# Distance slopes folded into the query scale and the fused add and maximum, in a two-block transformer forward pass

## The reference, cut to what matters

```python
def alibi_slopes(n_heads):
    return jnp.exp2(-8.0 * jnp.arange(1, n_heads + 1, dtype=jnp.float32) / n_heads)
# diff_attention
    sc = jnp.einsum('bqhmd,bkhmd->bhmqk', qi, k).astype(jnp.float32) * scale
    dist = jnp.abs(qpos[:, None] - kpos[None, :]).astype(jnp.float32)
    p = jax.nn.softmax(sc - slopes * dist, axis=-1)
    a = p[:, :, 0] - lam * p[:, :, 1]
# window_attention
    sc = jnp.where(valid, sc - slopes * dist.astype(jnp.float32), -jnp.inf)
```

## Time and profile before

| what | value |
|---|---|
| median of 3 runs | 2623.48 us (2622.71 to 2624.72) |
| the profiled execution: time, span | 2622.06 us, 2620.3 us |
| busy: PE, DVE, ACT, POOL | 2349.5 us (90%), 902.4 (34%), 518.4 (20%), 1046.5 (40%) |
| granted TensorE clock, mean | 0.975 |
| chain that ended last, by engine | PE 72%, DMA 14%, DVE 9%, issue 2% |
| POOL's high parts L480, low parts L483 | x216, 421.9 us; x222, 548.8 us |
| POOL's slope tables L529 (da), L533 (wa) | x8, 19.6 us; x16, 20.7 us |

### The profile page before, as it was taken

How to read it: one execution, slowest core, us unless ns; L and a number is a source line. 1 busy time by engine, 2 the same in 40 slices (tenths; PEclk the granted TensorE clock), 3 DMA queues, 4 the chain that set the end, 5 groups by cost and what they waited for, 6 DMA issues and landing times.

```text
span 2620.3 us, 26993 instructions
## 1 busy us (share of the span) xinstructions
PE 2349.5 (90%) x11209; PEld 1528.1 (58%) x11209; DVE 902.4 (34%) x1264; ACT 518.4 (20%) x1111; POOL 1046.5 (40%) x508
## 2 busy tenths in 40 slices
PE   5999988999998998889899999699988888888886
PEld 5777766888787875566578888343323333232322
DVE  2664855555302026655413353211010111101012
ACT  2253542211102014456411102000000000000001
POOL 5545754888778774444068886000000000000000
PEclk9999998999999999999999999799999999999998
DMA  4211221222222231111012227599999999999996
GB/s 163 80 49 65 81 97 64 97 97 97 97 97 82 97 97 33 33 65 49 1 65 97 97 97 282 238 418 417 417 417 417 416 417 416 417 417 418 418 417 276
DMA packets 172915, 531.60 MB, mean 203 GB/s; under 512 B 10018, under 2 KB 92155, under 8 KB 139515
## 3 DMA queue, kind: packets, MB, share of 16 engines
q1 hardware_dynamic: 169008, 521.17, 51.2%
q10 hardware_dynamic: 3787, 8.71, 0.9%
HBM read 525.66 MB, written 4.19 MB: 202 GB/s over the span
## 4 chain that ended last, share of the span: by engine, by line
PE 72%; DMA 14%; DVE 9%; issue 2%; ACT 1%; POOL 1%; ACTq 0%; SPq 0%; DVEq 0%; POOLq 0%
DMA arena<-in_w_exp_up 9%; PE ps L2062 9%; PE ps L1402 7%; PE ps L1404 7%; PE ps L1403 7%; PE ps L2035 7%; PE ps L1714 5%; DMA ring<-in_w_exp_up 4%; PE ps L1993 2%; PE ps L1418 2%; PE ps L1419 2%; PE ps L1420 2%; PE ps L1490 2%; PE ps L1492 1%; PE ps L1491 1%
## 5 line engine op out<-in xcount | busy, mean ns | idle before, releaser
L480 POOL TENSOR_TENSOR w_hi<-ring,one 128x1024 fp32r<-128x1024 f32 x216 | 421.9, 1953 | 481.7 <-PE ps L1404 179.3
L483 POOL TENSOR_TENSOR w_lo<-ring,w_hi 128x1024 fp32r<-128x1024 f32 x222 | 548.8, 2472 | 29.5 <-ACT w_hi L639 12.6
L579 POOL TENSOR_TENSOR arena<-arena 128x512 f32<-128x512 f32 x8 | 8.4, 1048 | 810.9 <-PE ps L2005 794.2
L1402 PE MATMUL ps<-h_hi,w_hi 128*128 128x512 f32 x656 | 255.9, 390 | 0.8 <-DVE arena L1234 0.8
L1404 PE MATMUL ps<-h_hi,w_lo 128*128 128x512 f32 x656 | 255.5, 389 | 0.0
L1403 PE MATMUL ps<-h_lo,w_hi 128*128 128x512 f32 x656 | 255.4, 389 | 0.0
L2035 PE MATMUL ps<-ring,arena 128*64 128x512 f32 x944 | 213.1, 595 | 41.6 <-DMA ring<-in_w_exp_up 40.1
L2035 PE MATMUL ps<-arena 128*64 128x512 f32 x944 | 213.0, 595 | 41.0 <-DMA arena<-in_w_exp_up 41.0
L2035 PEld LDWEIGHTS ps<-arena 128*64 128x64 f32 x944 | 71.5, 137 | 179.2 <-issue 178.9
L2035 PEld LDWEIGHTS ps<-ring,arena 128*64 128x64 f32 x944 | 71.2, 137 | 178.9 <-issue 176.8
L917 ACT ACTIVATE arena<-ps 64x1024 f32<-64x1024 f32 x32 | 30.8, 1010 | 568.1 <-PE ps L2035 568.1
(11 more groups left out here) (329 smaller groups left out, 4117.7 us busy)
## 6 DMA issues: line engine op xcount, KB each, us to landing
ring<-in_w_exp_gate SPq DMA_DIRECT2D x59, 1024.0 KB, 24.1
ring<-in_w_exp_up SPq DMA_DIRECT2D x59, 1024.0 KB, 25.4
arena<-in_w_exp_gate SPq DMA_DIRECT2D x59, 1024.0 KB, 24.1
arena<-in_w_exp_up SPq DMA_DIRECT2D x59, 1024.0 KB, 25.4
arena<-in_w_exp_down SPq DMA_DIRECT2D x54, 1024.0 KB, 18.7
ring<-in_w_exp_down SPq DMA_DIRECT2D x52, 1024.0 KB, 22.0
ring<-in_w_in SPq DMA_DIRECT2D x34, 1024.0 KB, 5.1
ring<-in_ffn_w_up SPq DMA_DIRECT2D x22, 1024.0 KB, 5.0
```

The lines of the kernel that those rows point to most:

```text
L480: nc.gpsimd.tensor_tensor(hi, w, one[:].unsqueeze(2).to_broadcast(list(w.shape)), ALU.mult).then_inc(w_high, 1)
L483: nc.gpsimd.tensor_tensor(lo, w, hi.bitcast(f32), ALU.subtract).then_inc(w_split, 1)
L1402: mm(o, w[0][:, k, :], h[0][:, k, 0:ntok], start=(k == 0), stop=False)
```

## The change

The score of a head is divided by the head's slope before, by a factor on the queries, and the fused instruction computes (score + (-distance)) times slope. In `da` the factor 0.125/slope is a constant of the eviction L765; in `wa` an eviction holds two heads (64 rows each), so its factor comes from a new tile `wq_scale`, filled by 16 memsets on DVE at the start. The tables of distances are read as they are; the sign of the subtraction and of the mask's fill is turned. The slope tables, their waits on POOL, and the calls of `split` between them go. The two distance tables are made one after the other, four halves later in POOL's order than the first was; behind them comes one `split(NH)` for all that is left. DVE waits for a table once per stage.

```diff
--- before.py
+++ after.py
@@ -43,6 +43,14 @@
 WA_UNIT = [[(i, 2 * qh + i // 2, kb) for i in range(4) for kb in WA_KB[2 * qh + i // 2]] for qh in range(2)]
 
 
+def da_slope(h):
+    return 2.0 ** (-8.0 * (h + 1) / DA_H)
+
+
+def wa_slope(h):
+    return 2.0 ** (-8.0 * (h + 1) / WA_H)
+
+
 def build(nc, I, out):
     f32, f32r, i32 = mybir.dt.float32, mybir.dt.float32r, mybir.dt.int32
     ALU, ACT, AX = mybir.AluOpType, mybir.ActivationFunctionType, mybir.AxisListType
@@ -63,6 +71,7 @@
         hT, hT_at = place(sb("hT", [P, KT, S]), KT * S)
         arena, arena_at = place(sb("arena", [P, ARENA]), ARENA)
         one = sb("one", [P, 1])
+        wq_scale = sb("wq_scale", [P, WA_H // 2])
         ident = sb("ident", [P, P])
         mean64 = sb("mean64", [P, P])
         head_col = sb("head_col", [P, 15])
@@ -152,8 +161,7 @@
         da_pt = ar(10240, 2, 4, 256)
         wdist = ar(12288, 384)
         dist = ar(30208, 896)
-        alibi = ar(13056, 2, 896)
-        walibi = ar(13312, 4, 384)
+        dtmp = ar(13056, 896)
         lamv = ar(10240, 4, 64)
         wa_q, wa_k, wa_v = ar(0, KT, S), ar(27136, WA_KV, S), ar(29184, TT, 256)
         o_wa = wa_q
@@ -520,46 +528,21 @@
             split(stage["da"] + 2)
 
             pool.wait_ge(x2_done, 8)
+            split(stage["da"] + 6)
             link(nc.gpsimd.iota(dist, pattern=[[-1, 896]], base=384, channel_multiplier=1,
                                 allow_small_or_imprecise_dtypes=True))
-            link(nc.gpsimd.tensor_scalar(alibi[:, 0, :], dist, 0.0, 2.0, ALU.max, ALU.mult))
-            link(nc.gpsimd.tensor_tensor(dist, alibi[:, 0, :], dist, ALU.subtract))
-
-            def slope(h):
-                nc.gpsimd.tensor_scalar(alibi[:, h % 2, :], dist, -(2.0 ** (-8.0 * (h + 1) / DA_H)), None,
-                                        ALU.mult).then_inc(al_done, 1)
-
-            def wslope(h):
-                nc.gpsimd.tensor_scalar(walibi[:, h % 4, :], wdist, -(2.0 ** (-8.0 * (h + 1) / WA_H)), None,
-                                        ALU.mult).then_inc(wal_done, 1)
-
-            slope(0)
-            slope(1)
-            for h, ahead in ((2, 3), (3, 4), (4, 5), (5, 7), (6, 8), (7, 9)):
-                split(stage["f1"] + ahead)
-                pool.wait_ge(sd_done, 8 * (h - 1))
-                slope(h)
+            link(nc.gpsimd.tensor_scalar(dtmp, dist, 0.0, 2.0, ALU.max, ALU.mult))
+            nc.gpsimd.tensor_tensor(dist, dist, dtmp, ALU.subtract).then_inc(al_done, 1)
             wtmp = ar(12672, 384)
             link(nc.gpsimd.iota(wdist, pattern=[[-1, 384]], base=P, channel_multiplier=1,
                                 allow_small_or_imprecise_dtypes=True))
             link(nc.gpsimd.tensor_scalar(wtmp, wdist, 0.0, 2.0, ALU.max, ALU.mult))
-            link(nc.gpsimd.tensor_tensor(wdist, wtmp, wdist, ALU.subtract))
-
-            link(nc.gpsimd.affine_select(out=wdist, in_=wdist, compare_op=ALU.is_ge, fill=-NEG, base=0,
+            link(nc.gpsimd.tensor_tensor(wdist, wdist, wtmp, ALU.subtract))
+
+            link(nc.gpsimd.affine_select(out=wdist, in_=wdist, compare_op=ALU.is_ge, fill=NEG, base=0,
                                          pattern=[[1, 384]], channel_multiplier=-1))
-            link(nc.gpsimd.affine_select(out=wdist, in_=wdist, compare_op=ALU.is_ge, fill=-NEG, base=256,
-                                         pattern=[[-1, 384]], channel_multiplier=1))
-            split(stage["f2"] + 1)
-            pool.wait_ge(sd_done, 64)
-            for h in range(4):
-                wslope(h)
-            split(stage["f2"] + 2)
-            for p in range(2, WA_H // 2):
-                pool.wait_ge(sw_done, 8 * (p - 1))
-                wslope(2 * p)
-                wslope(2 * p + 1)
-                split(stage["f2"] + min(p + 2, 8))
-
+            nc.gpsimd.affine_select(out=wdist, in_=wdist, compare_op=ALU.is_ge, fill=NEG, base=256,
+                                    pattern=[[-1, 384]], channel_multiplier=1).then_inc(wal_done, 1)
             split(NH)
 
             pool.wait_ge(x3_done, 8)
@@ -762,7 +745,7 @@
                 act.dma_start(lamv[:, i, :], I[n].partition_broadcast(P).rearrange("p a d -> p (a d)")).then_inc(in_small, 16)
             for n in range(8):
                 act.wait_ge(pj_ps, n + 1)
-                A(da_q[:, n, :], ps[:, n % 4, :], F.Copy, scale=0.125).then_inc(pjA, 1)
+                A(da_q[:, n, :], ps[:, n % 4, :], F.Copy, scale=0.125 / da_slope(n)).then_inc(pjA, 1)
             for n in range(16, J_F1):
                 if PJ[n] == "A":
                     act.wait_ge(pj_ps, n + 1)
@@ -777,7 +760,7 @@
             def wa_feature(j):
                 act.wait_ge(pj_ps, J_F1 + j + 1)
                 if j < 8:
-                    A(wa_q[:, j, :], ps[:, 3, :], F.Copy, scale=0.125).then_inc(pjA, 1)
+                    A(wa_q[:, j, :], ps[:, 3, :], F.Copy, scale=wq_scale[:, j:j + 1]).then_inc(pjA, 1)
                 else:
                     for i in range(2):
                         for o in range(2):
@@ -945,6 +928,8 @@
                 ins.then_inc(dve_c, 1)
                 dve.wait_ge(dve_c, n_[0])
 
+            for h in range(WA_H):
+                V.memset(wq_scale[64 * (h % 2):64 * (h % 2) + 64, h // 2:h // 2 + 1], 0.125 / wa_slope(h))
             dve.wait_ge(m2i_ready, 1)
             link(V.tensor_scalar(m2i, m2i, 3, None, ALU.bitwise_and))
             V.tensor_scalar(mask[:, 3, :], m2i, 0.0, NEG, ALU.is_gt, ALU.mult).then_inc(m2_ready, 1)
@@ -1153,15 +1138,15 @@
             for u in range(17):
                 if u < 16:
                     h = u // 2
-                    if u % 2 == 0:
-                        dve.wait_ge(al_done, h + 1)
+                    if u == 0:
+                        dve.wait_ge(al_done, 1)
                     if u >= 3:
                         dve.wait_ge(dt_ps, 2 * (u - 2))
                     for i in range(4):
                         qb = 2 * (u % 2) + i // 2
                         dve.wait_ge(sd_ps, 4 * u + i + 1)
                         V.tensor_tensor_reduce(out=da_e[:, u % 3, i, :], in0=ps[:, 4 + i, :],
-                                               in1=alibi[:, h % 2, 384 - P * qb:896 - P * qb], scale=1.0,
+                                               in1=dist[:, 384 - P * qb:896 - P * qb], scale=da_slope(h),
                                                scalar=-3e38, op0=ALU.add, op1=ALU.max,
                                                accum_out=mx[:, u % 2, i:i + 1]).then_inc(sd_done, 1)
                     dve.wait_ge(sd_done, 4 * u + 4)
@@ -1189,15 +1174,15 @@
             for u in range(17):
                 if u < 16:
                     p = u // 2
-                    if u % 2 == 0:
-                        dve.wait_ge(wal_done, 2 * p + 2)
+                    if u == 0:
+                        dve.wait_ge(wal_done, 1)
                     if u >= 3:
                         dve.wait_ge(wt_ps, 3 * (u - 2))
                     for i in range(4):
                         c0, c1 = wa_cols(u, i)
                         dve.wait_ge(sw_ps, 4 * u + i + 1)
                         V.tensor_tensor_reduce(out=wa_p[:, u % 3, i, c0:c1], in0=ps[:, 4 + i, c0:c1],
-                                               in1=walibi[:, (2 * p + i % 2) % 4, c0:c1], scale=1.0, scalar=-3e38,
+                                               in1=wdist[:, c0:c1], scale=wa_slope(2 * p + i % 2), scalar=-3e38,
                                                op0=ALU.add, op1=ALU.max,
                                                accum_out=mx[:, u % 2, i:i + 1]).then_inc(sw_done, 1)
                     dve.wait_ge(sw_done, 4 * u + 4)
```

## The result

| what | before | after |
|---|---|---|
| median of 6 runs each | 2623.36 us | 2634.35 us (2633.05 to 2636.52) |
| profiled execution: time, span | 2622.06, 2620.3 us | 2634.14, 2632.4 us |
| busy: PE, DVE, ACT, POOL | 2349.5, 902.4, 518.4, 1046.5 us | 2354.5, 896.1, 519.5, 1004.9 us |

The ratio is 1.004 (95% interval 1.003 to 1.005): the kernel became 11.0 us slower; the forecast was 10.2 us more. POOL has 42 us less to do, and the program takes longer.

The account below looks back on a forecast made before the run. PE matmul was taken as the bound, with POOL's splits having 1.1 us spare per half in the projections. 10.8 + 2.1 - 0.9 - 3.6 + 1.8 = 10.2 us more: median 2633.7 us, range 2627.3 to 2639.4.

Parts of the forecast that it names:

- The tables: Projections: both distance tables, 12.5 us on POOL, stand between the sixth and seventh splits, so PE loses 10.8 us.
- The clock: Behind the new stall in the projections: PE restarts at the lower clock level, 2.1 us more lost.
- my ends: For the clock behind the stall: a loss between nothing and twice 2.1 us.
- The norm: Norm: its last two DVE scalings no longer run beside POOL's table operations, 0.9 us gained; ends 0.5 and 1.
- Distance attention: Without slope tables and window table, splits hold DVE's scalings and PE less: 3.6 us gained; ends 2.5 and 5.
- Window attention: Splits in units 1, 7 and 10 now meet DVE's scalings, unit 12 gains: 1.8 us lost in all.
- What costs nothing: Query evictions with a tile factor, tiny memsets at the start, other evictions' constants: no cost, at most 0.7 us.
- hidden tables: Rival: PE has two halves ready at the seventh half, so no stall or clock loss; 2620.8 us, chance 8%.
- The port between DVE and POOL: Rival: port is the bound; without slopes the attention stages give back 8 us, not 2; total +4, 2627.5; chance 12%.
- The costly factor: Rival: a factor other than 1.0 adds half (0.3 us) to each fused attention instruction; 2650 us, chance 3%.

## Why the prediction was right

- **The tables (10.8 us forecast, 8.9 measured, 8.71 of it idle).** The mechanism and its place are as told: one stall at the seventh half, ended by the low part, recovered nowhere in the stage. The size was off by 1.9 us. Of that, 1.8 are the durations, 10.7 us for both tables where I had 12.5: I took them from 817.81 and 1088.86, where DVE works beside POOL. The same iota and clamp took 0.89 and 3.21 us at 854.43, not the 1.37 and 3.52 of the earlier trace rows, with DVE idle. What the change moves to another neighbourhood should be costed by a row from such a one. Moving the line back removed the whole loss.
- **The clock (2.1; 2.7).** The granted clock was at 0.50 up to 875.0, the level that it had behind the norm's gap, with 5.4 us of work in it where that had 4.3; the price is within my ends.
- **The norm (-0.9; -0.9).** DVE's last two scalings L942 take 0.75 us and PE stands 7.11 us, not 8.03. The sum has no term for the clock behind it, which takes 0.5 us of this back.
- **Distance attention (-3.6; -4.3).** PE's waits for the scalings are six, 18.9 us, as said (six, 19), so 4.2 us fewer. The seventh, 1.74 us at 1101, is gone; the two with a slope table behind the split are 3.83 and 3.30 us where they were 4.87 and 4.37, each some 0.1 us more than the 0.95 forecast; and the last, for which I had counted nothing, is 2.98 us where it was 3.30 (at 1129.12).
- **Window attention (+1.8; +3.9).** PE stands 2.32, 0.84 and 0.56 us in units 1, 7 and 10 (I had 2.3, 0.7, 0.7), and the 1.86 us of unit 12 are gone, as said. DVE's four scalings take 5.02, 5.12 and 5.06 us in those units. So the waits come to 1.8 us as forecast. The term that the step lacked is the clock: the eight transposes behind the 2.32 us gap take 1.94 us, those behind 0.84 and 0.56 take 1.09. After is 11.0 us behind where the first of these rows starts, and 12.7 some 4 us later: 1.7 us lost besides the gap. I had charged clock for the long stall only.
- **What costs nothing.** The fused instruction takes 0.69 us with the factor as without it, and the eviction with a factor from a tile 0.69 us as priced. Lines of after, columns as in the page:

```profile
L1148 DVE CUSTOM_DVE_ANT_0 arena<-ps,arena 128x512 f32<-128x512 f32 x64 | 40.6, 688 | 45.4 <-PE ps L1755 45.3
...
L763 ACT ACTIVATE arena<-ps,wq_scale 128x512 f32<-128x512 f32 x8 | 5.5, 687 | 8.6 <-PE ps L1736 8.6
```

The medians differ by 11.0 us, 0.8 from the 10.2 forecast, since the errors have opposite signs: -1.9 for the stall, +0.6 and +0.5 for the clock behind it and behind the norm, -0.7 and +2.1 in the attention stages; together +0.6, 10.8 for 10.2. The profiled executions differ by 12.1, of which 1.7 came ahead of anything changed. The parts had the right signs and places; that the total fits to a microsecond is luck.

**The rivals.** The tables were not hidden; the run with them at the old place gives the time with hidden tables, 2623.0 us, where the rival had 2620.8. Of the 2.2 us between them 0.9 are the norm, which the old place slows again; the rest has the sign of the window attention's clock, which the rival lacked too. The port between DVE and POOL is a real cost, but it belongs to the splits, which the change does not touch: removing the slopes and the window table gave 4 us in the distance attention, holding the splits 26 to 29 in all. The costly factor is not there: 0.69 us with it as without.

## What to carry to other kernels

Work that is taken from an engine with spare time gives nothing by itself; look at what the same edit does to the order in which that engine serves the others. Before moving a block on a producer engine, compare its length, taken from a row with the same neighbours, with the slack of one step at the new place. Where small scalings of DVE last exactly as long as an instruction of GpSimd beside them, and that engine has idle time, hold its work back by a wait: nine waits gave here what removing 42 us of work did not.

## What the runs showed of the hardware that was not expected

- One kernel's runs can fall into two groups: 2622.8 and 2627.2 for the tables in the gap, 2615.5 and 2620.2 with the window splits held, 4.4 and 4.7 us apart. A difference that would fit stands in the router in the profiles of two kernels, where the clock is at the lower level for all of 41 us in one and for three quarters of them in the other; that it parts the runs of one kernel is not shown. A median of a few runs can so be 4 us off by the draw; effects of that size need many runs and a look at the granted clock.
- POOL's own instructions took longer beside DVE's work: the iota 1.37 us, and 0.89 without; the clamp 3.52 and 3.21.
- A DVE scaling of two columns can take 2.33 us instead of 0.23, ten times as long, and the fused instruction of 512 columns with a PSUM input, beside the low part at 1012.32, is not slowed at all (0.69 us).
- A gap of PE of 2.3 us was followed by matmuls at the lower clock in the window attention, those of 0.84 and 0.56 us were not. The length of the gap alone does not decide: in the distance attention the eight transposes behind a gap of 3.27 us (1030.57) took 1.09 us, full speed, and those behind 3.83 us (999.21) took 1.97.
